# The experts' output product in eight slices of 128 columns in place of two of 512

## The reference

```python
def hierarchical_moe(h, ...):            # h: 2048 x 1024, 32 experts, 2 per token
    ...                                  # route; assignments sorted by expert, padded to blocks of 128
    def expert_block(args):
        xb, e = args                     # xb: 128 x 1024
        return (jax.nn.silu(xb @ exp_w1[e]) * (xb @ exp_w3[e])) @ exp_w2[e]
    ...
    y = y_buf[dest] * gate_sorted[:, None]
    out = jnp.zeros((n_tok, d)).at[tok_sorted].add(y)
```

## Time and profile before

| | us |
|---|---|
| median of 2 runs | 3212.54 |
| lowest, highest | 3210.64, 3214.44 |
| the profiled execution, span from its first to its last instruction | 3223.3 |
| TensorE busy in it | 2766.6 |
| VectorE, ScalarE, GpSimd busy | 1464.4, 1164.5, 924.0 |
| stage 6, from its first hidden product to the end | 2248.0 to 3223.3 |

### The profile page before, as it was taken

The page is one execution under the profiler, slowest core; times in us unless marked ns, Lnnn a source line. Parts: engine busy times, 40 slices in busy tenths (PEclk is TensorE's granted clock), DMA queues, the critical chain, the costliest instruction groups (busy, mean ns, idle before and its releaser), DMA issues. The chain is left out here.

```text
span 3223.3 us, 39417 instructions
## 1 busy us (share of the span) xinstructions
PE 2766.6 (86%) x11955; PEld 1955.2 (61%) x11956; DVE 1464.4 (45%) x2388; ACT 1164.5 (36%) x2065; POOL 924.0 (29%) x1270
## 2 busy tenths in 40 slices
PE   5894999999949777797999999972889989999987
PEld 1233644444434554556899988861667767777766
DVE  4565376221203232242354445421575676656674
ACT  3236121111112212122355444411554565555563
POOL 0000011000000000006045555553564575444574
PEclk8895999999979888895699999975899989999988
DMA  7455111121178787853011111112687687765783
GB/s 278 142 140 161 57 41 39 39 66 32 34 191 240 181 211 175 209 127 109 30 63 52 52 52 53 50 39 104 228 298 221 219 299 256 248 205 190 264 292 106
DMA packets 305307, 466.76 MB, mean 145 GB/s; under 512 B 27048, under 2 KB 193600, under 8 KB 298336
## 3 DMA queue, kind: packets, MB, share of 16 engines
q1 hardware_dynamic: 223410, 384.14, 37.8%
q0 software_dynamic: 16976, 39.52, 5.3%
q10 hardware_dynamic: 64832, 41.96, 4.7%
HBM read 367.33 MB, written 113.81 MB: 149 GB/s over the span
## 5 line engine op out<-in xcount | busy, mean ns | idle before, releaser
L748 PE MATMUL ps_proj<-sb_hT,sb_win 128*128 128x512 f32 x768 | 335.5, 596 | 7.6 <-DVE sb_rot L837 6.0
L2012 POOL TENSOR_TENSOR sb_w<-sb_raw_w,sb_w2h 128x2048 fp32r<-128x2048 f32 x64 | 296.1, 4680 | 108.9 <-ACT sb_w2h L1928 108.9
L2072 PE MATMUL ps_bh<-sb_w,sb_bxTh 128*128 128x512 f32 x736 | 305.6, 415 | 0.0
L1341 POOL MEMSET sb_pr<- 128x1026 int32 x1 | 1.0, 959 | 909.6 <-POOLq L185 909.6
L748 PEld LDWEIGHTS ps_proj<-sb_hT,sb_win 128*128 128x128 f32 x768 | 145.6, 191 | 189.5 <-issue 182.6
L2072 PE MATMUL ps_bh<-sb_w1h,sb_bxTh 128*128 128x512 f32 x368 | 163.8, 445 | 80.8 <-DVE sb_w L1856 57.6
L1138 DVE TENSOR_TENSOR sb_ab<-sb_ab,ps_prod 128x512 f32<-128x512 f32 x64 | 44.0, 688 | 359.1 <-ACT sb_ab L1114 359.1
L1620 DVE CUSTOM_DVE_ANT_0 sb_pr<-ps_S,sb_mask 128x640 f32<-128x640 f32 x128 | 105.5, 824 | 216.6 <-PE ps_S L1469 216.5
L1489 PE MATMUL ps_O<-sb_v,sb_pt 128*128 128x64 f32 (+1 forms) x1280 | 176.3, 293 | 0.0
L1548 ACT COPY sb_pt<-ps_PT 128x512 f32<-128x512 f32 x128 | 74.7, 584 | 275.4 <-PE ps_PT L1475 275.3
L1489 PEld LDWEIGHTS ps_O<-sb_v,sb_pt 128*128 128x128 f32 x1280 | 173.7, 215 | 0.0
(11 more groups left out here) (281 smaller groups left out, 5929.7 us busy)
## 6 DMA issues: line engine op xcount, KB each, us to landing
sb_raw_w<-in_exp_w SPq DMA_DIRECT2D x90, 2048.0 KB, 11.2
sb_ada<-in_ada_w SPq DMA_DIRECT2D x16, 1536.0 KB, 7.8
scr_filt<-sb_fout ACTq DMA_DIRECT2D x128, 128.0 KB, 2.5
sb_yh<-scr_filt SPq DMA_DIRECT2D x32, 512.0 KB, 11.1
scr_hy_y<-sb_sp SPq DMA_DIRECT2D x32, 512.0 KB, 7.0
sb_yx<-scr_hy_y SPq DMA_DIRECT2D x32, 512.0 KB, 8.0
scr_hy_v<-sb_yx SPq DMA_DIRECT2D x64, 256.0 KB, 4.3
sb_sp<-scr_hy_v SPq DMA_DIRECT2D x32, 512.0 KB, 6.7
```

The costliest lines, as they stand in the source:

```text
L748: ins = pe.matmul(mp[:, (NQ + n) % 4, :], w[:, pc % 3, k, (ct % 2) * P:(ct % 2 + 1) * P], g.hT[:, k, c * 512:(c + 1) * 512], start=(k == 0 ...
L1341: pool.memset(fill, NOWHERE).then_inc(setup, 1)
L2012: pool.tensor_tensor(cols(w2[par])[:, cs], cols(raw2[par])[:, cs], cols(w2h[par])[:, cs].bitcast(F32), ALU.subtract).then_inc(lo2, 1)
L2072: ins = pe.matmul(out, a[:, k, :], b(k), start=(k == 0 and j == 0), stop=(k == n - 1 and j == 2))
```

## The change

TensorE's `output` goes through the 1024 output columns in eight slices of 128 in place of two of 512. Each slice is contracted in full (4 x 3 matmuls) before the next. Slices 0 to 3 go into the first PSUM bank at offsets 0, 128, 256 and 384, slices 4 to 7 into the second. `ym` goes up after slices 3 and 7, so the other engines see the same two signals. Nothing else is changed.

```diff
                 pe.wait_ge(glo, n + 1)
                 pe.wait_ge(y_ok, n)
-                for half in range(2):
-                    cs = slice(half * 512, (half + 1) * 512)
-                    split_product(yp[:, half, :], gTh, gT, lambda k: w2h[par][:, k, cs], lambda k: w2[par][:, k, cs], FT)\
-                        .then_inc(ym, 1)
+                for part in range(KT):
+                    cs = slice(part * P, (part + 1) * P)
+                    ps = slice(part % 4 * P, (part % 4 + 1) * P)
+                    ins = split_product(yp[:, part // 4, ps], gTh, gT, lambda k: w2h[par][:, k, cs], lambda k: w2[par][:, k, cs], FT)
+                    if part % 4 == 3:
+                        ins.then_inc(ym, 1)
```

## The result

The changed kernel takes 3375.07 us (median of 2 runs, 3369.61 to 3380.53) for 3212.54 before: 1.0514 times as long, 95% interval 1.0478 to 1.055. The forecast was 3348 in a range of 3300 to 3480. The profiled execution has a span of 3378.5 us for 3223.3, +155.2.

The account below looks back on a forecast made before the run. The prediction took TensorE, busy 86% of the span, as the bound, with waits where experts have one block. Its terms, 225 - 70 - 33 + 15 - 2 = +135 us, carried to the 3212.5 median, gave 3348 us, range 3300 to 3480.

Parts of the forecast that it names:

- The main term: TensorE's output product: 96 matmuls at 0.110 us, 10.56 us for 5.67, +4.89 in each of 46 blocks, +225 us.
- The Trainium skill's two rules: Price of a 128-column matmul: load rule 107 ns, +4.6 us a block; issue-gap rule 81 ns, +2.1 us.
- The first hidden term: TensorE's gaps before the next first hidden product, at most 4.77 us, are covered by the longer output product: -70 us.
- the residual: Where one-block experts follow one another, late weight transfers leave gaps up to 1.8 us, at most 18 times: +15 us.
- The second hidden term: First hidden products slowed by a clock that fell in the gap before them return to full speed: -33 us.
- the short gaps: 13 TensorE waits of about 0.95 us before first hidden products, after VectorE's late sb_bxT operation.
- the long ones: 18 TensorE gaps of 2.7 to 4.8 us before first hidden products, put on VectorE's first part of sb_w.
- VectorE's late signal for half 0: The output product's first semaphore comes 2.5 us later, ahead of w1's low parts; costs nothing, margin 3 us.
- The end: Two last output products end 9.8 us later, partly beside a 6.15 us scatter wait; the end moves by 8: -2 us.
- The clock rival: Sparse output products drop TensorE's clock to 0.50 in each block: +658 us, 3871 us; chance 0.07.
- Full fp32 price: Each short float32r matmul runs as two fp32 records, 0.236 us: +674 us, 3887 us; chance 0.12.
- Not slower: Weight loads in the output product fully hidden, 0.073 us per matmul: -7 us, 3205 us; chance 0.07.

Follow-up runs that it names:

- first128: The kernel before with only half 0 of the output product in slices of 128 columns, half 1 in one of 512: 3250.34 us, ratio 1.0132.
- second128: The kernel before with only half 1 of the output product in slices of 128 columns, half 0 in one of 512: 3273.53 us, ratio 1.019.

## Why the prediction was right, point by point

**The main term, 46 x 4.89 = +225.** Right in mechanism, 2% low in size per matmul: 0.1112 to 0.112 us for 0.110, which makes 46 x 5.12 = 235.5. The 64-column run bears out the reason given, as far as a width can: at full clock the spacing is the same at 64 and at 128 columns. That the fixed cost is the weight load and nothing else was argued from rows, not tried.

**The Trainium skill's two rules.** The trace has the warm matmuls of 64 and of 128 columns 0.112 us apart. By the Trainium skill's page "TensorE: Matmul & The Clock Gate", section "LDWEIGHTS (loading the stationary operand)", a load takes its 128 columns over 1.2, 107 ns: close. The 81 ns of its section "Back-to-back issue gap" is not met by float32r operands here.

**The first hidden term, -70 for gaps, and the residual, +15.** Together -55; measured -54.1. The fill is right in mechanism. That the residual came out is luck: the prediction gave it to the weights' transfer, at up to 18 places. The chain of the changed kernel has the transfer ahead of one gap, the one of 3.0 us at 2400.49:

```profile
2389.58 8.44 DMA sb_raw_w<-in_exp_w
...
2399.12 1.24 DVE sb_w L1856
...
2400.49 1.57 PE ps_bh L2072 x4
```

The others are 2.5 and 1.25 us once each and 0.1 to 0.7 at experts' first blocks. 8.6 us of them in 16 waits, the 2.5 included, have no releaser in the profile.

**The second hidden term, -33 for slow starts.** Measured -27.9 over all starts; the two blocks at the stage's start, by themselves, lost 1.0 us more than before. Slow starts fell from 17 to 4.

**What the gaps were.** The prediction saw that VectorE's sb_bxT beside GpSimd's 9.19 us is late before the short gaps, and put the long ones on sb_w's first part. The runs with two and four pieces show that both hang on GpSimd's long operations: the short gaps for their whole length, the 18 long ones for some two fifths of it (57.6 us in the kernel before, 35.1 with four pieces).

**VectorE's late signal for half 0.** Held to cost nothing, with 3 us of margin. The pair first128 and second128 shows no cost of 15 us; a smaller one is not separated from what else the order of the halves does.

**The end, -2.** The step that failed. It took the last product at the same 0.110 as all others; it runs at 0.211, +9.6 us, at a clock of 0.54. The clock rival was put at 0.07 as a matter of all blocks or none. What it says holds for one product in the place where the dense hidden products are missing between two sparse ones, and for 64 columns in the loop.

**The sum.** Spacing +10, last product +10 and slow starts +5 make the miss of 25 us in the stage (160 for 135).

**The rivals.** Full fp32 price is out: single records, 0.112. Not slower (loads hidden, 0.073 per matmul) is out: 0.112 at 128 columns. The clock is in, but elsewhere and small.

## What to carry to other kernels

Below 256 columns a float32r matmul that changes its stationary operand cost 0.112 us here at full clock, at 128 columns and at 64, so slicing an output more finely only adds loads: two and four slices were equal, eight cost 5%, sixteen 48%, of which about half came from the clock. Added work on the bounding engine is first paid out of that engine's holes, so read the gaps before pricing it, and expect more of its price once someone closes them (208 us for 160 in the stage here, of some 245). A VectorE operation between SBUF tiles that takes four times its own length (2.99 us for 0.68) was here the sign of a long GpSimd operation beside it. Cutting that into two pieces gave 1.3%, into four 1.6%; eight lost 1.6%.

## What the runs showed of the hardware that I had not expected

The clock fell with TensorE never idle, and how sparse the stream was decided it: 128-column matmuls at 0.112 us kept it at 1.00 through 10.7 us in each block, 64-column ones at the same spacing lost it after 3.0 to 6.3 us in 45 of 46. The product of the row shown then took 36.9 us for 21.5 at its loads' rate.

In all three kernels with eight slices in both halves the last product ran at half clock (20.29, 20.32 and 19.90 us for 96 matmuls), though the 45 before it did not. With one sparse half per product (first128, second128) the last one kept the clock: 60 matmuls in 8.42 and 8.36 us.

GpSimd's subtraction of one expert's w2 costs 9.3 us in two operations and 14.1 in sixteen (450.5 us over 32 experts), beside the same VectorE work. A VectorE operation that meets such a row of short operations is not sure to be let in between two of them: it waited up to 6.6 us beyond its own 0.68.
